# Seven-product FFN on one NeuronCore: weight sums moved to VectorE, three additions moved to accumulating DMAs

## The reference, cut to what matters

```
h = rms(x) * (1 + scale_f) + shift_f
a, g = split(h @ ffn_w_in)              # 2048 x (5632 + 5632)
x = x + gate_f * rms((silu(a) * g) @ ffn_w_out, norm_g[3])     # 5632 x 2048
```

## Time and profile before

| | |
|---|---|
| median of the runs shown | 2750.97 us (2750.62 to 2753.04) |
| the profiled execution's own time | 2752.95 us |
| its span, first to last instruction | 2751.2 us |
| TensorE busy, of the span | 2601.0 us, 95% |
| VectorE busy | 2315.4 us, 84% |
| ScalarE busy | 1473.4 us, 54% |
| GpSimd busy | 762.5 us, 28% |
| mean granted clock | 0.981 |

### The profile page before, as it was taken

The page is one execution under the profiler, slowest core; times in us unless marked ns, Lnnn a source line. Parts: engine busy times, 40 slices in busy tenths (PEclk is TensorE's granted clock), DMA queues, the critical chain, the costliest instruction groups (busy, mean ns, idle before and its releaser), DMA issues.

```text
span 2751.2 us, 34264 instructions
## 1 busy us (share of the span) xinstructions
PE 2601.0 (95%) x11952; PEld 2119.2 (77%) x11952; DVE 2315.4 (84%) x2616; ACT 1473.4 (54%) x1965; POOL 762.5 (28%) x542
## 2 busy tenths in 40 slices
PE   9999999999999999999999999998888878888898
PEld 8888888888888878888887778876566656666687
DVE  6889688887888797767869887888999999999798
ACT  6555666656566664555554544555444444444344
POOL 0021031313230000800000000005777777677200
PEclk9999999999999999999999999999999999999999
DMA  9668688887888867565567668875444444444685
GB/s 323 206 220 277 212 269 299 275 284 260 280 277 295 273 216 264 182 211 173 176 215 239 217 214 274 314 242 183 161 161 138 143 155 147 152 160 138 231 297 199
DMA packets 278675, 615.57 MB, mean 224 GB/s; under 512 B 19948, under 2 KB 21168, under 8 KB 276368
## 3 DMA queue, kind: packets, MB, share of 16 engines
q1 hardware_dynamic: 273696, 583.53, 63.5%
q0 software_dynamic: 4704, 30.33, 3.0%
q10 hardware_dynamic: 144, 0.01, 0.0%
HBM read 601.18 MB, written 13.39 MB: 223 GB/s over the span
## 4 chain that ended last, share of the span: by engine, by line
PE 73%; DVE 17%; issue 3%; POOL 2%; DMA 2%; ACT 2%; SPq 0%; DVEq 0%; POOLq 0%; ACTq 0%
PE ps L786 72%; DVE w_lo L3368 11%; DVE down_x L3381 1%; DMA w_raw<-in_ffn_w_in 1%; ACT w_hi L1525 1%; POOL arena L3761 1%; DVE arena L3402 1%; DMA w_raw<-in_w_in 1%; DVE w_lo L2363 1%; DVE down_rows L3381 1%; POOL arena L3763 1%; POOL arena L3750 0%; PE ps L1449 0%; DVE arena L2358 0%; POOL w_raw L3763 0%
## 5 line engine op out<-in xcount | busy, mean ns | idle before, releaser
L1525 ACT ACTIVATE w_hi<-w_raw 128x1024 fp32r<-128x1024 f32 (+1 forms) x802 | 831.9, 1039 | 949.9 <-PE ps L786 731.7
L786 PE MATMUL ps<-w_hi,hop_part 128*128 128x512 f32 x3624 | 1164.3, 393 | 34.4 <-DVE w_lo L3368 27.2
L2363 DVE TENSOR_TENSOR w_lo<-w_raw,w_hi 128x1024 fp32r<-128x1024 f32 x617 | 773.8, 1257 | 304.6 <-ACT w_hi L1525 300.5
L786 PEld LDWEIGHTS ps<-w_hi,hop_part 128*128 128x128 f32 x3624 | 682.5, 188 | 200.4 <-DVE w_lo L3368 43.6
L786 PE MATMUL ps<-w_lo,hop_part 128*128 128x512 f32 x1812 | 707.2, 390 | 0.0
L786 PEld LDWEIGHTS ps<-w_lo,hop_part 128*128 128x128 f32 x1812 | 341.4, 188 | 68.3
L3368 DVE TENSOR_TENSOR w_lo<-arena,w_hi 128x1024 fp32r<-128x1024 f32 (+1 forms) x160 | 309.8, 1973 | 10.3 <-ACT w_hi L1525 9.4
L786 PE MATMUL ps<-w_hi,hid_hi_part 128*128 128x512 f32 x736 | 287.5, 391 | 0.0
L786 PE MATMUL ps<-w_hi,hid_lo_part 128*128 128x512 f32 x736 | 286.4, 389 | 0.0
L786 PE MATMUL ps<-w_lo,hid_hi_part 128*128 128x512 f32 x736 | 286.4, 389 | 0.0
L2358 DVE SCALAR_TENSOR_TENSOR arena<-arena,cs 128x768 f32<-128x768 f32 x240 | 246.2, 1026 | 0.3
(11 more groups left out here) (372 smaller groups left out, 3080.5 us busy)
## 6 DMA issues: line engine op xcount, KB each, us to landing
arena<-in_ada_w SPq DMA_DIRECT2D x256, 384.0 KB, 5.3
w_raw<-in_w_up SPq DMA_DIRECT2D x128, 512.0 KB, 4.5
w_raw<-in_w_down SPq DMA_DIRECT2D x128, 512.0 KB, 4.7
w_raw<-in_w_gate SPq DMA_DIRECT2D x128, 512.0 KB, 4.2
w_raw<-in_ffn_w_in SPq DMA_DIRECT2D x112, 512.0 KB, 4.6
w_raw<-in_ffn_w_out SPq DMA_DIRECT2D x88, 512.0 KB, 4.6
w_raw<-in_w_out SPq DMA_DIRECT2D x64, 512.0 KB, 4.8
w_raw<-in_wide_columns SPq DMA_DIRECT2D x64, 512.0 KB, 3.9
```

Source lines behind the costliest of these rows:

```text
L786: return nc.tensor.matmul(o, w, r, start=start, stop=stop, skip_group_check=True)
L1525: return nc.scalar.activation(o, i, ACT.Copy, scale=scale)
L2363: V.tensor_tensor(w_lo[:, j % LEAD, :, 0:cols], w_raw[:, j % RAW, :, 0:cols], w_hi[:, j % LEAD, :, 0:cols].bitcast(F32), ALU.subtract).the ...
```

## The change

What moves from which engine to which:

- The first and second weight sums go from GpSimd to VectorE (`weight_sums`), with one place for the first (`T_SUMS`) instead of two.
- The fourth sum becomes a DMA from SBUF to SBUF that adds what it reads to its destination (`fourth_sum`, 256 KB written), issued from GpSimd's queue. Signs of the activation sums change to match.
- A down unit's low part is no longer subtracted by VectorE. ScalarE writes minus the high part (`down_minus`, a second pass over the unit), and an accumulating DMA adds the unit as loaded (`down_sum`, 512 KB). The ring has 4 places.
- A visit's bank is copied out by ScalarE (`visit_out`), and an accumulating DMA adds the copy to `ACC_TOK` (`visit_sum`, 256 KB).
- The fourth piece is made one step later, after the next group's first sum on VectorE, ahead of its first piece on ScalarE. On SyncE `load_down(s + 1)` stands ahead of `load_pair(s + 3)` and waits for the `down_sum` of unit s - 1.

```
-E_RING = 3
+E_RING = 4
...
         for s in range(GROUPS):
-            if s < 2:
-                sp.wait_ge(sem["lo_ready"], R_FFN * 8 + 15 + s)
-            else:
-                sp.wait_ge(sem["down_lo"], HEADS + s - 1)
-            load_down(s)
+            if 1 <= s < VISITS - 1:
+                sp.wait_ge(down_lo[(s - 1) % 2], S5_DMAS + 16 * ((s - 1) // 2 + 1))
+                load_down(s + 1)
             if s + 3 < GROUPS:
                 sp.wait_ge(sem["lo_ready"], forms(s + 2))
                 load_pair(s + 3)
...
+        def down_minus(u):
+
+            copy(down_weights(u, 1), w_raw[:, 2 + u % 2], scale=-1.0).then_inc(sem["down_hi"], 1)
+
+        def visit_out(v):
+
+            bank = SPARE_BANK if v - (VISITS - SHIFT) in (0, 2) else VISIT_BANK
+            act.wait_ge(sem["visit_used"], HEADS + 2 * v + 2)
...
+            elif v >= 2:
+                act.wait_ge(visit_added[v % 2], S5_ADDS + 16 * (v // 2))
+            copy(visit_tile(v), PS[bank][:]).then_inc(sem["visit_drained"], 1)
...
-        for s in range(-1, GROUPS + 2):
-            if 0 <= s - 2 < VISITS:
-                down_hi(s - 2)
+        for s in range(-1, GROUPS + SHIFT + 1):
+            if s > SHIFT:
+                visit_out(s - SHIFT - 1)
+            if 0 <= s < GROUPS:
+                form_hi(s, 3)
...
+            if 0 <= s - 1 < VISITS:
+                down_hi(s - 1)
             next_hi(s, 1)
...
             next_hi(s, 2)
-            next_hi(s, 3)
+            if 0 <= s - 1 < VISITS:
+                down_minus(s - 1)
...
+        def weight_sums(g, k):
+
+            raw = PAIR_RAW[g % 2]
+            if k == 0:
+                dve.wait_ge(pair_in[g % 2], 16 + 32 * (g // 2 + 1))
...
+                    dve.wait_ge(sem["lo_ready"], forms(g - 1, 3))
+                m = V.tensor_tensor(T_SUMS, raw[:, 1], raw[:, :, 0], ALU.subtract)
+            else:
+                dve.wait_ge(sem["sums_made"], HEADS + 4 + 2 * g + 1)
+                m = V.tensor_tensor(raw[:, 1, 0], T_SUMS[:, 0], raw[:, 1, 1], ALU.subtract)
+            m.then_inc(sem["sums_made"], 1)
...
+        def visit_sum(v):
+
+            d, n, t = visit_of(v)
+            pool.wait_ge(sem["visit_drained"], HEADS + v + 1)
+            pool.dma_start(ACC_TOK[:, t, n * COLS:(n + 1) * COLS], visit_tile(v), accum_op=ALU.add).then_inc(visit_added[v % 2], 16)
+
+        def fourth_sum(g):
+
+            raw = PAIR_RAW[g % 2]
+            pool.wait_ge(sem["lo_ready"], forms(g, 1))
+            pool.wait_ge(sem["sums_made"], HEADS + 4 + 2 * g + 2)
+            pool.dma_start(raw[:, 0, 1], raw[:, 1, 0], accum_op=ALU.add).then_inc(sem["fourth_made"], 16)
+
+        def down_sum(u):
+
+            pool.wait_ge(sem["down_hi"], HEADS + u + 1)
+            pool.dma_start(down_weights(u, 1), w_raw[:, 2 + u % 2], accum_op=ALU.add).then_inc(down_lo[u % 2], 16)
```

More of the change, by code:

```diff
@@ L414, in two_blocks @@
     down_rows = nc.alloc_sbuf_tensor_at("down_rows", [P, 2, UK, COLS], F32R, offset=place["row_store"])
+    down_const = nc.alloc_sbuf_tensor_at("down_const", [P, 2, UK, COLS], F32R, offset=place["const"] + P * 4)
     gain_scratch = nc.dram_tensor("gain_scratch", [2, D], F32, kind="Internal")
@@ L742, in _ @@
         load_pair(0)
+        for u in range(2):
+            sp.wait_ge(sem["lo_ready"], R_FFN * 8 + 15 + u)
+            load_down(u)
         sp.wait_ge(sem["hop_ready"], HOP[7] + KT + 4)
@@ L759, in _ @@
                 sp.wait_ge(sem["lo_ready"], forms(GROUPS))
+                for i in range(2):
+                    sp.wait_ge(visit_added[i], S5_ADDS + 8 * VISITS)
             ada(ADA_LAST, j, G_FFN, ada_cols(G_FFN))
@@ L3426, in _ @@
                 sums_lo(j - 7)
[L3427 to L3431, removed]
-            if 0 <= s - 2 < VISITS:
-                down_lo(s - 2)
+        for s in range(-1, GROUPS + 2):
             end = super_end(s)
+            if s + 1 < GROUPS:
+                weight_sums(s + 1, 0)
+            if 0 <= s < GROUPS:
+                form_lo(s, 3)
             if end is not None:
                 end_step(end, 0)
+            if s + 1 < GROUPS:
+                weight_sums(s + 1, 1)
             next_lo(s, 0)
@@ L3450, in _ @@
                 end_step(end, 3)
-            next_lo(s, 3)
-            if end is not None:
                 end_step(end, 4)
+            if s == GROUPS + 1:
+                next_lo(s, 3)
+        for i in range(2):
+            dve.wait_ge(visit_added[i], S5_ADDS + 8 * VISITS)
         dve.wait_ge(sem["end_pool"], 4 * SUPERS)
@@ new lines, in down_sum @@
+        def down_sum(u):
+            pool.wait_ge(sem["down_hi"], HEADS + u + 1)
+            pool.dma_start(down_weights(u, 1), w_raw[:, 2 + u % 2], accum_op=ALU.add).then_inc(down_lo[u % 2], 16)
+        pool.wait_ge(sem["cleared"], 2)
+        for s in range(-1, GROUPS + SHIFT + 1):
+            if s > SHIFT:
+                visit_sum(s - SHIFT - 1)
+            if after_end(s) is not None:
+                end_sum(after_end(s), 2)
+            if s + 1 < GROUPS:
+                fourth_sum(s + 1)
+            if after_end(s) is not None:
+                end_sum(after_end(s), 3)
+            if super_end(s) is not None:
+                end_sum(super_end(s), 0)
+                end_sum(super_end(s), 1)
+            if 0 <= s - 1 < VISITS:
+                down_sum(s - 1)
```

74 lines of the change are left out of this document (27 added, 47 removed).

## The result

The changed kernel takes **2850.81 us** (2848.36 to 2859.41), the kernel before beside it 2751.64: ratio 1.0366, 95% interval 1.0343 to 1.0388, +99 us where 23 were forecast. The sign was right; the size was not. The time lies in the wide range (2670 to 2860), but above the range of the case that I chose, 2733 to 2820. The profiled execution's span is 2846.6 us, 95.4 more than before.

A forecast was written before the change was run, and what follows sets the result against it. The prediction took VectorE, hindered by GpSimd's additions, to bound the seven-product stage. 64 steps x 0.31 = +20 us and +3 at the stage's end gave 2776 profiled, 2774 us as median; range 2670 to 2860.

The forecast's parts named there:

- the case that I chose: Seven-product stage: added bytes cost double a copy's, 10.8 us a step, 2774 us, range 2733 to 2820; chance 0.50.
- the two thirds named: VectorE in the stage: its busy share should fall to near two thirds, with subtractions at 1.21 us.
- the double price: Accumulating DMAs: each written byte costs twice a copy's, source and destination both being read; 5.5 to 6.3 us a step.
- I take 10.8 us against 10.49 now: Stage's pitch: value taken from DMA engines' 10.2 to 11.0 and the ring's 11.2 us a step.
- The DMA engines' sum: DMA engines in the stage: 4.7 us of loads plus added bytes at double price, 10.2 to 11.0 us a step.
- the ring: Stage: one chain of waits over three steps through SyncE, VectorE, ScalarE and two accumulating DMAs, 11.2 us a step.
- the size of the landings: Stage's two accumulating DMAs in the ring: fixed part plus transfer doubled for contention, 5.8 + 8.6 = 14.4 us.
- the prediction's own formula: Stage's pitch from waits: (15.7 + 1.5 + 14.4) / 3 = 10.5 us, plus 0.7 for chunk ends, 11.2.
- +3: Stage's end: VectorE and SyncE wait until the last visit's sum has landed, +3 us.
- Copy price: Rival for accumulating DMAs: the second read is hidden, 9.6 us a step, 2697 us; chance 0.33.
- slower than double: Rival for accumulating DMAs: three times a copy's cost, 13.4 us a step, 2940 us; four times, 3125; chance 0.14.
- Everything fits: Rival for the stage: landings are overlapped and TensorE bounds at 7.6 us a step, 2568 us; chance 0.03.

The follow-up runs named there:

- Kernel 8: Changed kernel with down units' low parts, visits' sums and the fourth sum all on VectorE, no accumulating DMA left: 2689.81 us, ratio 0.9778.
- Experiment 4: Changed kernel with the visits' sums back on VectorE, straight from PSUM, without ScalarE's copy and its DMA: 2844.65 us, ratio 1.0342.
- kernel 3: Changed kernel with down units' low parts back on VectorE, one subtraction replacing ScalarE's minus pass and the accumulating DMA: 2659.66 us, ratio 0.9668.
- pair first: Edit issuing the pair's loads ahead of the down load on SyncE's queue: 2787.37 us on the changed kernel, 2739.70 us on kernel 3.
- experiment 2: Changed kernel with its three accumulating DMAs made plain copies, their additions left out: 2744.57 us in a single run.
- kernels 3 and 6: The second of these is kernel 3 with the pair's loads ahead of the down load on SyncE's queue: 2739.70 us, ratio 0.9954.

## Why the prediction was right and wrong

**Right: the bound before, and what frees VectorE.** VectorE was hindered by GpSimd's weight sums. Its 1024-wide low parts went from 1965 ns to 1287 and 1222 in the changed kernel, its busy share in the stage to 0.57, under the two thirds named because the step is longer. Kernel 8 shows the same with more work on VectorE.

**Right: the double price.** Added bytes cost 0.471 x 600 / 51.2 steps = 5.5 us a step, the lower end of "5.5 to 6.3", and twice the copies' price for a byte. The Trainium skill ("Collectives: The Full Stack", section "The bandwidth ceiling: the fold count and why AG ≠ RS ≠ AR") puts the halved rate of sums in collectives down to their two source reads. The trace agrees in the ratio, 188 to 376 GB/s; that the reads are the cause here no run shows. The loads' own share rose as well, from 4.7 to 5.3 us a step, which the prediction had left unchanged. In all it is 10.8 us, inside "10.2 to 11.0" and equal to the forecast pitch, but by one term at its lower end and one too small; and it isn't what sets the pitch.

**Wrong: "I take 10.8 us against 10.49 now".** This is the step that failed: it measured 11.71, and the sum's +20 us was +77. The DMA engines' sum gave 10.2 to 11.0, the ring 11.2, and I took a value between, below my own ring. Two lower bounds aren't averaged; the larger stands. That alone is 0.4 us a step, 26 us. Experiment 4 shows that it wasn't the DMA engines' work: a share of 0.79 in place of 0.93 at nearly the same pitch.

**Wrong: the size of the landings.** The fourth sum's was priced 5.8 us and took 7.6; the pair's was priced 6.0 and took 6.4 to 6.8; the down sum's was priced 8.6 and took 7.8. By the prediction's own formula, with these put in (the pair at 6.6, 2.1 later than its 4.5), (15.7 + 2.1 + 15.4) / 3 + 0.7 = 11.8 us against 11.71 measured. That this comes so close is partly luck, since the formula is that of a ring which isn't there as drawn. The doubling of the transfer for contention was a little too much for the 512 KB DMA and far too little for the 256 KB one, which took nearly as long to land, 7.6 us to 7.8. These sizes account for the other 0.5 us or so.

**Incomplete: the ring itself.** I drew one ring over three steps and didn't look for shorter ones through the same landings. The fourth ring by itself gives 7.6 + 3.4 = 11.0 us and at a chunk's end more, the down ring 11.1 in the rows; each holds the fourth low part in about half of the steps. What each would give without the other was not measured. Here the wrong drawing cost little, since all three are near one another. It costs more in judging a repair: by the prediction's ring the loads' order should matter only through the down sum's landing, and on kernel 3, where that landing is gone, "pair first" lost 80 us.

**The ends.** "+3" for what waits at the stage's end was 11 in it and 7.4 behind it. In the timeline TensorE has two stalls there where it had one of 10.18 us:

```profile
2661.88 1.19 PE L796 MATMUL ps<-down_rows,hid_hi_part 128*128 128x512 f32 x2 [11.49 <-DMA down_rows<-w_raw]
...
2668.64 1.22 PE L796 MATMUL ps<-down_const,hid_hi_part 128*128 128x512 f32 x2 [3.87 <-DMA down_const<-w_raw]
```

They are 5 us more. The other 6 us in the stage weren't found. The 7.4 behind the last visit's sum are probably VectorE and SyncE starting the next stage late; no run tested it.

**The rivals.** *Copy price* (2697) and *slower than double* (2940) both fell with experiment 2: the price of a byte is two copies. That the time stands in the stated range is owed to the range's width: it is 31 us above the 2820 that the chosen case was given. *Everything fits* fell with the waits. In the copy case the forecast said 9.6 us a step; with real copies it was 10.13, again by the landing (6.2 where 4.4 was priced).

## What to carry to other kernels

When work moves from an engine to a DMA, price its latency before its bandwidth: follow every path on which its landing leads back to its own next issue, divide each by the steps it spans, and take the largest; a ring of one step hides easily behind a longer one. When you cut a ring by reordering, look for the wait that the new order creates (a buffer freed later, a load that can no longer start early) and price that too. Give an accumulating DMA only sums for which nobody waits, such as the visits' here, and keep on an engine those that the next issue needs.

## What the runs showed beyond that

- Three accumulating DMAs within SBUF in each step (256, 512 and 256 KB) moved 188 GB/s at full share of the DMA engines where the same copies moved 376, and an issue held GpSimd's queue for 0.86 us against 0.54. With only some of them left the rate was 140 (the fourth sum alone) to 191 (fourth and down sum, kernel 4).
- The loads' own rate at full share fell from 334 GB/s to 294 in the change (80.07 MB at 45.4% of 600 us). The additions beside them aren't enough to explain it: with all of them still there and only the pair's loads first it was 321, in kernel 3 it was 341, and with no accumulating DMA at all (kernel 8) 321. Its cause is open.
- The fourth sum's DMA of 256 KB landed in 3.6 us at best, in 4.4 in the median in kernel 3, and in 7.6 in the change, where three accumulating DMAs and three loads came in every step. The order of issue alone moved the median from 4.4 to 6.1 us (kernels 3 and 6) at the same number of bytes a step.
- A DMA share of 0.93 or 0.97 isn't proof of a bound: with a quarter of the added bytes gone the pitch stayed near 11.8 and the share fell from 0.93 to 0.79.
- GpSimd's additions hindered VectorE's two-operand subtractions in SBUF (1.97 us for 1.22), and its issuing of accumulating DMAs hardly did (1.29 and 1.22).
